# A hybrid streaming encoder on one core: the tensors in SBUF are laid out at other addresses

## The reference

```
h    = rms_norm(x, w_norm1);  proj = h @ w_in                      # 1024 -> 2048
conv = gb * conv3(gc * a);    attn = windowed GQA with sinks;      gmlp = u * (W_s v + b)
x    = x + concat(rms(conv), rms(attn), rms(gmlp)) @ w_out
h2   = rms_norm(x, w_norm2)
ff   = square(relu(h2 @ w_ff1))                                    # 1024 -> 4096
x    = x + ff @ w_ff2                                              # 4096 -> 1024
```

## The kernel before, in words

| tensor | before | after |
|---|---|---|
| `w_hi` | 16512 (0) | 164128 (32) |
| `w_lo` | 32896 (0) | 180512 (32) |
| `w_raw` | 49280 (0) | 196896 (32) |
| `base_n`: `xn`, `S`, `kn`, `vn`, `s1`, `ring[0]` | 57472 (0) | 205088 (32) |
| `base_r`: `kcT`, `wsT`, `squares` | 69760 (0) | 217376 (32) |
| `base_x`: `x`, `s2`, and `s3` 18432 on | 75904 (0) | 16512 (0) |
| `h_all`, `ring_all`, `b_all`, `z_all` | 112768 (0) | 53408 (32) |
| `base_u`: `q`, `u_sb`, `part` | 186496 (0) | 127136 (32) |
| `ring[3]` | 195712 (0) | 136416 (32) |
| `base_c`: `aT`, `qn`, `qT`, `yat`, `sq6` | 214144 (0) | 154784 (32) |
| `ident` and the small ones behind it | 223440 (16) | 223520 (32) |

## Time and profile before

### The profile page before, as it was taken

How to read it: one execution, slowest core, us unless ns; L and a number is a source line. 1 busy time by engine, 2 the same in 40 slices (tenths; PEclk the granted TensorE clock), 3 DMA queues, 4 the chain that set the end, 5 groups by cost and what they waited for, 6 DMA issues and landing times.

```text
span 2220.0 us, 34007 instructions
## 1 busy us (share of the span) xinstructions
PE 2181.7 (98%) x13190; PEld 1962.9 (88%) x13190; DVE 1582.0 (71%) x2603; ACT 913.4 (41%) x1724; POOL 134.0 (6%) x227
## 2 busy tenths in 40 slices
PE   7999999999999999999999999999999999999998
PEld 7988878999999978888899887789999999888886
DVE  5326875788777777877862378668877777877767
ACT  5123532456555623233331235234555555223233
POOL 5011010000000000000040101010000000000002
PEclk9999999999999999999999999999999999999999
DMA  6101012335454786646221110133555558856363
GB/s 175 52 25 47 20 44 79 130 148 214 173 207 171 282 310 246 214 146 228 86 73 39 39 33 20 48 115 118 189 184 202 175 205 313 304 189 225 141 222 114
DMA packets 213456, 330.09 MB, mean 149 GB/s; under 512 B 14620, under 2 KB 97856, under 8 KB 213296
## 3 DMA queue, kind: packets, MB, share of 16 engines
q1 hardware_dynamic: 209600, 321.66, 40.8%
q0 software_dynamic: 2832, 3.10, 0.6%
q10 hardware_dynamic: 864, 3.15, 0.4%
HBM read 212.02 MB, written 115.64 MB: 148 GB/s over the span
## 4 chain that ended last, share of the span: by engine, by line
PE 89%; DVE 6%; ACT 2%; issue 1%; DMA 1%; SPq 0%; POOL 0%; DVEq 0%; ACTq 0%; POOLq 0%
PE ps L2060 28%; PE ps L2062 28%; PE ps L2061 28%; PE ps L2116 1%; DVE x L1492 1%; DMA ff_ops<-row_op 1%; DVE h_all L1474 1%; PE ps L2220 0%; PE ps L2159 0%; PE ps L2201 0%; DVE xn L1355 0%; DVE w_lo L1340 0%; DVE mx L1439 0%; PE ps L2240 0%; DVE S L1446 0%
## 5 line engine op out<-in xcount | busy, mean ns | idle before, releaser
L2060 PE MATMUL ps<-h_all,w_hi 128*128 128x288 f32 (+1 forms) x1408 | 439.9, 312 | 1.0 <-DVE q L1645 1.0
L2062 PE MATMUL ps<-h_all,w_lo 128*128 128x288 f32 (+1 forms) x1408 | 438.5, 311 | 0.0
L2061 PE MATMUL ps<-h_all,w_hi 128*128 128x288 f32 (+1 forms) x1408 | 438.0, 311 | 0.0
L2060 PE MATMUL ps<-w_hi,h_all 128*128 128x512 f32 (+1 forms) x720 | 273.2, 379 | 6.3 <-DVE x L1492 5.3
L2062 PE MATMUL ps<-w_hi,h_all 128*128 128x512 f32 (+1 forms) x720 | 266.5, 370 | 0.0
L2060 PEld LDWEIGHTS ps<-h_all,w_hi 128*128 128x128 f32 x1408 | 264.6, 188 | 2.0 <-DVE q L1645 1.5
L2061 PE MATMUL ps<-w_lo,h_all 128*128 128x512 f32 (+1 forms) x720 | 265.9, 369 | 0.0
L2061 PEld LDWEIGHTS ps<-h_all,w_hi 128*128 128x128 f32 x1408 | 264.7, 188 | 0.0
L2062 PEld LDWEIGHTS ps<-h_all,w_lo 128*128 128x128 f32 x1408 | 264.6, 188 | 0.0
L2061 PE MATMUL ps<-w_lo,ring_all 128*128 128x512 f32 x544 | 211.6, 389 | 0.0
L2062 PE MATMUL ps<-w_hi,ring_all 128*128 128x512 f32 x544 | 211.6, 389 | 0.0
(11 more groups left out here) (252 smaller groups left out, 4153.9 us busy)
## 6 DMA issues: line engine op xcount, KB each, us to landing
ff_ops<-row_op SPq DMA_DIRECT2D x128, 512.0 KB, 3.3
w_raw<-in_w_ff SPq DMA_DIRECT2D x128, 256.0 KB, 3.7
ring_all<-ff_ops SPq DMA_DIRECT2D x32, 1024.0 KB, 8.4
ring<-ff_ops SPq DMA_DIRECT2D x32, 1024.0 KB, 8.7
ff_raw<-q SPq DMA_DIRECT2D x96, 256.0 KB, 3.4
b_all<-in_w_ff SPq DMA_DIRECT2D x24, 1024.0 KB, 12.2
w_raw<-in_w_in SPq DMA_DIRECT2D x64, 256.0 KB, 3.6
ring<-ff_raw SPq DMA_DIRECT2D x12, 1024.0 KB, 5.5
```

Source lines behind the costliest of these rows:

```text
L2060: pe.matmul(out, sh, mh, start=first, stop=False)
L2061: pe.matmul(out, sh, ml, start=False, stop=False)
L2062: return pe.matmul(out, sl, mh, start=False, stop=last)
```

## The change

The address of nearly every tensor in SBUF is changed, as in the table above. `x` comes first, then 32 bytes left free (`OFF`), then `h_all` and the regions behind it, then 16 + 32 more bytes left free, then `w_hi`, `w_lo`, `w_raw` and the region of `xn`, then that of `kcT`, then the small tensors as before. `ring[3]` starts another 64 bytes into its region. No instruction is added, removed or moved on any engine: each has the same operations on the same tensors, shapes and waits in the same order. Line numbers below the edit differ by one.

```diff
@@ -76,6 +76,7 @@
 SB = FB - CB
 HR = ROWS // 2
 HG = HR // 2
+OFF = 32
 FORD = ("P1", "P2", "P5", "P6", "P7", "P4", "P3")
 PORD = ("P1", "P2", "P5", "P7", "P6", "P4", "P3")
 FOPS = len(FORD) * SB
@@ -145,18 +146,9 @@
             return nc.alloc_sbuf_tensor_at(name, shape, dt, offset=at, align_bytes=16)
 
 
-        wh = place("w_hi", [P, 8, 512], F32R)
-        wl = place("w_lo", [P, 8, 512], F32R)
-        raw = place("w_raw", [P, RAW, 512])
-
-        base_n = cursor[0]
-        xn = place("xn", [P, 2, D])
-        gN = place("gN", [P, D])
-        base_r = cursor[0]
-        cursor[0] += 6144
-
         base_x = cursor[0]
         x = place("x", [P, T, D])
+        cursor[0] += OFF
         h_all = place("h_all", [P, 2, KD, ROWS], F32R)
         hTh, hTl = h_all[:, 0], h_all[:, 1]
         base_u = cursor[0]
@@ -177,8 +169,14 @@
         qT = place("qT", [P, G4 * P], at=base_c + 2048)
         yat = place("yat", [P, G4, P], at=base_c + 4096)
         sq6 = place("sq6", [P, 6, P], at=base_c + 6144)
-        cursor[0] = base_c + 9296
-
+        cursor[0] = base_c + 9312 + OFF
+        wh = place("w_hi", [P, 8, 512], F32R)
+        wl = place("w_lo", [P, 8, 512], F32R)
+        raw = place("w_raw", [P, RAW, 512])
+
+        base_n = cursor[0]
+        xn = place("xn", [P, 2, D])
+        gN = place("gN", [P, D])
         S = place("S", [P, 2, HEADS * P], at=base_n)
         pT = place("pT", [P, HEADS * P], at=base_n + 8192)
         wnat = place("wnat", [P, 4, P], at=base_n)
@@ -189,6 +187,9 @@
         kn = place("kn", [P, 2, P], at=base_n + 8192)
         vn = place("vn", [P, 2, 256], at=base_n + 9216)
         yg = place("yg", [P, 256], at=base_n + 11264)
+
+        base_r = cursor[0]
+        cursor[0] += 6144
 
         base_h = base_u - 2 * KD * ROWS * 4
         ring_all = place("ring_all", [P, 2, KD, ROWS], F32R, at=base_h)
@@ -205,7 +206,7 @@
         ring = [place("ring0", [P, HALF, 2, 512], F32R, at=base_n)[:],
                 ring_all[:, :, 0:4, 0:512].rearrange("p h j n -> p j h n"),
                 ring_all[:, :, 4:8, 0:512].rearrange("p h j n -> p j h n"),
-                place("ring3", [P, HALF, 2, 512], F32R, at=base_u + 9216)[:]]
+                place("ring3", [P, HALF, 2, 512], F32R, at=base_u + 9216 + 2 * OFF)[:]]
         y_rows = [b_all[:, h, k:k + 2, 0:512] for h in range(2) for k in range(0, KD, 2)]
         y_rows.append(xn[:, 0, :].rearrange("p (k n) -> p k n", k=2))
         b11 = raw[:]
```

## The result

The changed kernel takes 2244.55 us (median of 4 runs, 2243.17 to 2247.5) against 2222.14 before (2221.64 to 2223.01): ratio 1.0102, 95% interval 1.0085 to 1.0119. It is slower by 22.4 us, outside the range of the prediction by 2.6 us and on the side that was thought less likely. Its profiled execution took 2245.07 us, its span 2242.8.

A forecast was written before the change was run, and what follows sets the result against it. The prediction took TensorE, matmul count times pitch, as the bound. Terms of 0 for matmuls, VectorE and ScalarE, and DMAs on a 2220.0 us span plus 2.2 around it gave 2222.2, forecast 2222, range 2196 to 2242.

The forecast's parts named there:

- What bounds the kernel: Whole kernel: TensorE, busy 2181.7 of 2220.0 us, so the time is a count of matmuls times their pitch.
- the one on matmuls: The 11,328 large matmuls on TensorE: new start addresses change their pitch by 0.
- rival (a): Large matmuls: weight load and moving stream collide in SBUF depending on their starts; faster, 14 us, 2208; chance 0.32.
- a near end: Bound kept beside the 0 for large matmuls: -2.5 or +2.5 ns per matmul.
- the fixed part: Time per large matmul beyond 0.4167 ns a column: 13.2 ns at 512 columns, 144 us in all.
- Rival (b): Moving streams starting off 64 bytes need one more aligned piece, 3.3 ns per matmul; slower, 33 us, 2255; chance 0.23.
- VectorE, ScalarE, DMAs: Vector and scalar instructions and transfers at new addresses: 0 each, with 0.8 us and 0.2 us either way kept.

The follow-up runs named there:

- m1: Measuring kernel, only matmuls, distance between stationary and moving starts varied in one SBUF layout: 512 columns read 226.7 ns at 0, 233.5 at 128, 234.1 at 96.
- m3: Measuring kernel, 24 matmuls of 512 columns at every pair of moving and stationary starts, 0 to 240 bytes in steps of 16: no pair under 226.7 ns.
- m4b: Measuring kernel, 288, 384 and 256 columns at distances 0 to 240 bytes: 288 columns read 131.7 ns at 0 and 133.3 at 128.
- m2: Measuring kernel, stationary operands of 128, 64 or 32 columns and alternating starts: at distance 0 they read 226.7, 230.0 and 231.7 ns.
- m6: Measuring kernel, 512-column groups behind three matmuls of 16 or 128 columns: at distance 16 bytes 233.3 and 226.7 ns, at 240 bytes 228.3 behind both.
- m5: Measuring kernel, 288 and 384 columns at shifted moving starts, 512 at stationary 16 and 240: 512 columns read 232.9 and 228.5 ns.

## Why the prediction was wrong

**What bounds the kernel** was right: TensorE alone, by count times pitch. The loss is all in pitches. Summed over the times from each matmul's start to the next, before to after: 512 columns on `h_all` 405.2 to 412.7 us, on `ring_all` (with `z_all`) 394.2 to 402.3, on the other ring buffers 305.0 to 307.6, 384 columns 305.0 to 309.9, 288 columns 580.3 to 580.7, 256 columns 53.0 to 52.7, all small matmuls and waits 158.3 to 158.2. Together some 23 us, and the span is 22.8 us longer.

**The step that failed** is the one on matmuls: "I take 0, the value that rows 6 and rows 9 show." Rows 6 were read as proof that a pitch doesn't depend on where the stationary operand lies, since they pass from `ring_all` to another ring buffer. But these two, like all buffers of the large products in that kernel, leave the same rest after division by 512. The rows varied the distance by whole multiples of its period, and so could show nothing of the rest that the change alters. The table of addresses ahead of the prediction had that fact; it was used under rival (a) as room for a gain only. Rows 9 compared weight loads by their recorded duration, which isn't the pitch. What the runs showed in place of the 0: 232.4 ns against 226.5 on `ring_all`, 175.8 against 173.3 at 384 columns, and nothing in sum at 288, where the halves of the products on `h_all` changed places.

**The value it should have had**: the one row before in which the rest did change was the earlier trace rows, 2.5 ns for one half of the 288-column products against the other. It was kept as a near end, and rightly read as an address or a bank. m1 has 1.7 ns for 288 columns, 2.4 for 384 and 5.7 to 6.7 for 512, so its transfer to the longest products was short by more than half. 3360 matmuls of 512 columns at 5.7 ns (`h_all`, `ring_all`), 672 at 2.3 (`ring[3]`) and 1728 of 384 at 2.4 would give 19 + 2 + 4 = 25 us; measured 22.4. Most of the difference lies on `h_all`, which lost 7.5 us where 1728 x 5.7 ns make 9.8.

**Rival (a)** had the mechanism's form (the distance between two starts) and the wrong sign: distance 0 is the best, not one among equals, and the fixed part of 13.3 ns fell at no pair of m3 for 512 columns. **Rival (b)**, that came out nearest in time, had a wrong mechanism: with both starts 32 bytes off, m1 reads 226.7 ns, and after the change `ring[0]` does too; P6, which it left as before, has its first half at 601.76 - 600.16 = 1.60 us, slower than P5's 1.58. Over all 26 blocks P6's first half reads 133.1 ns and P7's 131.8, at the same distance of 160, where m4b has 131.8; so for 288 columns too the distance isn't the whole account, and what parts P6 from P7 stays open. **VectorE, ScalarE, DMAs** at 0 were right: 1.9 and 0.4 us of busy time, none of it in waits, and `row_op`'s store lands after 3.3 us as in the earlier trace rows. By the Trainium skill ("DMA: Bandwidth & Descriptors", how a descriptor splits into AXI transactions) the prediction had an estimate of 1.5% more for that store. Its 68 and 69 beats are those of a piece of 2048 bytes; these stores have 4096 bytes per partition (512 KB over 128), for which the same rule gives an estimate of 132 and 133 beats, 0.8%. Neither can be seen at the resolution of 3.3 us.

**The range** ended at 2242, since half of rival (b) had been left out. Its lesson is the width: an unknown price that acts on 11,328 matmuls is worth 11 us per ns, and the earlier trace rows showed that nanoseconds were at stake.

## What to carry to other kernels

Where weight loads and moving streams of 384 or 512 columns alternate back to back, as here, lay the two operands out on multiples of 32 bytes so that their starts are equal modulo 256, for every product of the stage, and pad in multiples of 256. Other lengths have other rows (256 columns read 120.0 ns at distance 0 and 113.8 at 64), so measure the length that you have. Before a row is taken as proof that something doesn't matter, ask whether it varied the very thing that the change varies. A buffer inserted ahead of others moves every later start, so a layout edit of a few bytes can cost 1% with nothing to see in waits or order; the pitch in the timeline shows it.

## What the runs showed of the hardware

- The pitch of a stream of 128x128 loads and 512-column matmuls (float32r in the kernel, f32 in the profile) lay between 226.7 and 234.2 ns by the start addresses, and went up to 236.7 with the moving start at an odd multiple of 16 (m3).
- Its steady values often lie 6.67 ns apart: 226.7 and 233.3 (m1, m3), and 240.0 for loads of 32 columns 32 bytes off (m2). That is 16 periods of the 2.4 GHz level; why wasn't found.
- At a distance of 16 bytes it keeps either 226.7 or 233.3 ns, whichever it was led into by what ran before (m6). At 240 bytes it read 226.7 in m1 and m3 and 228.3 to 228.5 in m5 and m6.
- A narrower load made such a stream slower at distance 0 (230.0 ns with 64 columns, 231.7 with 32, 226.7 with 128) and faster at 128 (229.6, 230.5, 232.4); at 32 bytes, loads of 32 columns took 239 ns where 128 columns took 233 (m2).
